# Smaller first transfers in another order, a first weight tile split by chunks, and twelve turns of the identity on TensorE

## The chip, the cores and the metric

The kernel runs on one core of one Trainium2 chip. Its time is the device time of one execution in microseconds (us), and lower is better. The engines of the core are TensorE (PE in the profile), VectorE (DVE), ScalarE (ACT), GpSimd (POOL) and SyncE (SP), which issues most of the transfers. Each runs its own list of instructions in order and waits for the others on semaphores.

## The reference

Two decoder layers over 256 tokens of width 1024, all in float32. Layer 0 mixes tokens by native sparse attention (NSA), layer 1 by multi-head latent attention, and each is followed by a SwiGLU channel mixer. RMS norms stand around every part:

```python
for i in range(DEPTH):                       # DEPTH = 2
    u = rms_norm(h, ln_mix_pre[i])
    m = nsa_mixer(u, ...) if i == 0 else mla_mixer(u, ...)
    h = h + rms_norm(m, ln_mix_post[i])
    u = rms_norm(h, ln_ffn_pre[i])
    h = h + rms_norm(swiglu(u, w_gate, w_up, w_down), ln_ffn_post[i])
```

The NSA mixer begins with `h @ w_in` (keys, values, gates and queries), and turns queries and keys by rotary angles computed from the positions. Only this beginning is touched by the change.

## The kernel before

**Token and weight tiles.** The 256 tokens are two token tiles, t = 0 and 1, with 128 tokens on the partitions. The width is eight chunks of 128. Weights stream through three slots: weight tile n lies in `raw[n % 3]` (128x2048), four chunks of 512 columns for this stage. Tiles 0 and 1 hold the first key/value block (chunks 0 to 3 and 4 to 7), tiles 2 and 3 the second, 4 and 5 the third; then come the gates and the rest.

**Split in two parts.** For float32 accuracy each operand is a rounded high part and a remainder. ScalarE writes `w_hi` (`split_hi`, L229), VectorE writes `w_lo = raw - w_hi` (`split_lo`, L241), and a product is three matmuls (`product`, L256 to L258). `split_hi` counts `hi_ready`, `split_lo` counts `lo_ready`, on which TensorE (`take`) and the load of a slot's next tile wait.

**Activations.** `u = h * gain` is made on VectorE (`pre_norm`, L412), in halves of 512 columns. TensorE turns each half with four transposes (`turn_pe`, L467), ScalarE copies the high part (`turn_act`, L476) and VectorE the low part (`turn_dve`, L482). The norm's root isn't in u: squares and a square root on ScalarE (`pre_root`, L323, L311, L312) and the inverse on VectorE (`pre_invert`, L378 to L384) give a factor that is applied when results leave PSUM (L1166).

**First block on TensorE** (`first_block`): turn both halves of token tile 0; chunks 0 to 7 for token tile 0, with the first half of token tile 1 turned before chunk 6 and the second after chunk 7; chunks 0 to 7 for token tile 1. Then `kv_block(1)` takes tiles 2 and 3 (24 matmuls each), 16 transposes of the keys and values follow (they need the copies at L1166), and `kv_block(2)` takes tiles 4 and 5.

**Order on the other engines.** It is the order in which the code is written. VectorE computes the rotary angles after the inverse roots (L1645 to L1664), ScalarE takes sine and cosine (L1313, L1314), then the high part of tile 3, then the copies at L1166. SP issues x (token tile 0), the gain, tile 0, x (token tile 1), tiles 1 and 2; the load of tile 3 waits for w_lo of tile 0. GpSimd makes the identity for the transposes (L644, L646) after two small transfers.

Of the kernel before, what the change touches and what calls it, by code (L numbers as in the profile page):

```python
# [25 lines left out]
P = 128  # L26
# [80 lines left out]
def trunk(nc, x, positions, inv_freq, gains, lat_gain, nsa_w_in, pe_k, pe_v, w1_k, w1_v, w2_k, w2_v, nsa_w_out,  # L107
          mla_w_in, w_q_up, w_kv_up, mla_w_out, w_gate_up, w_down, out):
    with ExitStack() as ctx:
# [165 lines left out]
        def project_wide(pe, n, stat_hi, stat_lo, first, start, stop, last_of=None):  # L275

            s = n % 3
            for t in range(T):
# [6 lines left out]
                if last_of is not None and t == 0:  # L285
                    last.then_inc(sem(f"acc_done{last_of}"), 1)
# [21 lines left out]
        def root(tally, s, t, k, name):  # L308
# [4 lines left out]
                           bias=stat(s, t, k + 2)).then_inc(sem(f"{name}{s}"), 1)  # L313

        def pre_root(tally, s, t):

            act = tally.eng
            for half in range(2):
                if s == 0:
                    act.wait_ge(sem(f"x_loaded{t}"), 16)  # L320
# [6 lines left out]
        def post_root(tally, s, t, n):  # L327

            act = tally.eng
            if t == 0:  # L330
                act.wait_ge(sem(f"acc_done{s}"), 1)
            else:
                wait_used(act, n)
            for half in range(2):
# [57 lines left out]
        def post_invert(tally, s, t):  # L392
            tally.eng.wait_ge(sem(f"post_root{s}"), t + 1)
# [164 lines left out]
        def _(sp):  # L558
# [80 lines left out]
        def _(pool):  # L639
            pool.memset(eps[:], EPS).then_inc(sem("eps"), 1)  # L640
            pool.dma_start(pos_i[:], positions).then_inc(sem("pos_loaded"), 16)
            pool.dma_start(invf[:], inv_freq.to_broadcast([P, 16])).then_inc(sem("pos_loaded"), 16)

# [3 lines left out]
                               pattern=[[-1, P]], channel_multiplier=1).then_inc(sem("ident"), 1)  # L647

# [66 lines left out]
        def _(pe):  # L715
# [43 lines left out]
            def first_block(s, n):  # L759
# [7 lines left out]
                for t in range(T):  # L767
                    for k in range(KC):
                        if k % 4 == 0:
                            pe.wait_ge(sem(f"u{s}_lo"), 2 * t + k // 4 + 1)  # L770
                            if t == 0:
                                take(pe, n + k // 4)
                        if t == 0 and k == 6:
# [7 lines left out]
                    if t == 0:  # L781
                        last.then_inc(sem(f"first_block{s}"), 1)
# [1092 lines left out]
```

## Time and profile before

| | |
|---|---|
| median of 3 runs | 796.91 us (796.35 to 799.35) |
| profiled execution | span 796.9 us from the first to the last instruction; nothing further is recorded around it |
| TensorE busy | 715.8 us (90%) |
| VectorE busy | 438.9 us (55%) |
| ScalarE busy | 369.6 us (46%) |
| mean granted TensorE clock | 0.951 of full speed |
| chain that ended last | PE 73%, DVE 14%, ACT 6%, issue 5%, DMA 1% |
| moved from memory | 109.54 MB, mean 139 GB/s |

A matmul is pipelined with the next one, so its duration is longer than the distance between two starts: 0.39 us against 0.23 for 512 columns at the full clock. Where two matmuls are compared, the distance of their starts counts. The rows name a line of the kernel; `x4` at the end of a row merges four like instructions. The idle time in brackets is that engine's, ahead of the row, with what ended it.

### The profile page before, as it was taken

To read this page: it belongs to the slowest core of one execution; us is meant where nothing else is said; L and a number is where in the kernel's file an instruction comes from. 1 tells how busy PE (TensorE), PEld (TensorE's weight loads), DVE (VectorE), ACT (ScalarE), POOL (GpSimd) and SP (SyncE) were. 2 spreads that over 40 slices of the span, in tenths; PEclk is the share of its full clock that TensorE was granted. 3 is DMA by queue.
4 is the path that set the end of the run, shared out by engine and by line. 5 is a ranking of instruction groups with operands and counts; after the bars stand their busy time and mean duration, and the time that the engine had idled before them with its cause. 6 is when DMAs were issued, how large, how long until landed. Compare 5 with 4: busy or idle time off the path is not lost.

```text
span 796.9 us, 10320 instructions
## 1 busy us (share of the span) xinstructions
PE 715.8 (90%) x3601; PEld 599.7 (75%) x3601; DVE 438.9 (55%) x898; ACT 369.6 (46%) x678; POOL 75.5 (9%) x63
## 2 busy tenths in 40 slices
PE   3999899938969999999997997887969999999994
PEld 2899787827857888888886787876757888888883
DVE  4666566495386555444556554555285455444553
ACT  6564554505355444334445445445355444334432
POOL 6000011080020000000002001112420000000000
PEclk9999899969989999999999979999999999999998
DMA  9563110431045546554453322242333545654421
GB/s 319 202 210 103 56 40 13 159 109 50 1 152 173 177 163 217 208 201 158 158 190 133 113 87 86 87 134 78 106 127 111 185 161 213 209 206 158 158 106 53
DMA packets 55918, 110.95 MB, mean 139 GB/s; under 512 B 4225, under 2 KB 15537, under 8 KB 55889
## 3 DMA queue, kind: packets, MB, share of 16 engines
q1 hardware_dynamic: 54544, 106.24, 39.5%
q0 software_dynamic: 1344, 4.35, 1.6%
q8 instruction: 15, 0.25, 0.1%
q14 instruction: 15, 0.11, 0.0%
HBM read 109.54 MB, written 1.05 MB: 139 GB/s over the span
## 4 chain that ended last, share of the span: by engine, by line
PE 73%; DVE 14%; ACT 6%; issue 5%; DMA 1%; DVEq 0%; SPq 0%; ACTq 0%
PE bank L256 22%; PE bank L257 21%; PE bank L258 21%; DVE w_lo L241 2%; PE bank L804 2%; PE bank L827 1%; DVE u L412 1%; ACT w_hi L229 1%; PE bank L740 1%; DMA raw<-in_nsa_w_in 1%; PE bank L810 1%; DVE lat_g L1569 1%; DVE nmax L1521 1%; DVE s_sb L1516 1%; DVE h L402 1%
## 5 line engine op out<-in xcount | busy, mean ns | idle before, releaser
L241 DVE TENSOR_TENSOR w_lo<-raw,w_hi 128x2048 fp32r<-128x2048 f32 (+5 forms) x105 | 205.9, 1981 | 65.5 <-ACT w_hi L229 65.4
L256 PE MATMUL bank<-w_hi,act_lo 128*128 128x512 f32 (+3 forms) x592 | 230.7, 390 | 10.9 <-DVE w_lo L241 9.8
L258 PE MATMUL bank<-w_hi,act_hi 128*128 128x512 f32 (+3 forms) x592 | 225.0, 380 | 0.0
L257 PE MATMUL bank<-w_lo,act_hi 128*128 128x512 f32 (+3 forms) x592 | 224.6, 379 | 0.0
L229 ACT ACTIVATE w_hi<-raw 128x2048 fp32r<-128x2048 f32 (+5 forms) x98 | 170.3, 1763 | 20.4 <-PE bank L258 18.6
L256 PEld LDWEIGHTS bank<-w_hi,act_lo 128*128 128x128 f32 x592 | 115.4, 195 | 33.3 <-issue 6.1
L258 PEld LDWEIGHTS bank<-w_hi,act_hi 128*128 128x128 f32 x592 | 115.3, 195 | 20.9
L257 PEld LDWEIGHTS bank<-w_lo,act_hi 128*128 128x128 f32 x592 | 115.5, 195 | 18.7
L1163 ACT ACTIVATE hidT_hi<-bank 128x512 fp32r<-128x512 f32 x22 | 13.1, 597 | 176.3 <-PE bank L740 176.3
L1490 DVE TENSOR_TENSOR hidT_lo<-bank,hidT_hi 128x512 fp32r<-128x512 f32 x22 | 15.2, 692 | 139.9 <-ACT hidT_hi L1163 139.9
L256 PE MATMUL bank<-w_hi,hidT_lo 128*128 128x512 f32 x176 | 69.2, 393 | 3.0 <-DVE hidT_lo L1490 3.0
L257 PE MATMUL bank<-w_lo,hidT_hi 128*128 128x512 f32 x176 | 69.3, 394 | 0.0
L258 PE MATMUL bank<-w_hi,hidT_hi 128*128 128x512 f32 x176 | 68.4, 389 | 0.0
L241 POOL TENSOR_TENSOR w_lo<-raw,w_hi 128x2048 fp32r<-128x2048 f32 x9 | 41.2, 4579 | 270.7 <-ACT w_hi L229 269.7
L1220 ACT ACTIVATE s_sb<-s_sb,nmax 128x128 f32<-128x128 f32 (+1 forms) x72 | 32.4, 451 | 43.4 <-DVE nmax L1521 43.0
L804 PE MATMUL bank<-big,qT 96*128 96x256 f32 (+4 forms) x128 | 46.9, 454 | 5.5 <-DVE big L1613 3.0
L827 PE MATMUL bank<-big,pT 128*128 (+1 forms) x288 | 42.4, 277 | 7.6 <-DVE qs L541 5.0
L827 PEld LDWEIGHTS bank<-big,pT 128*128 128x128 f32 x288 | 40.0, 203 | 10.5 <-DVE qs L541 5.4
L1163 ACT ACTIVATE pT<-bank 128x256 f32<-128x256 f32 (+2 forms) x64 | 25.9, 405 | 37.0 <-PE bank L810 36.8
L256 PEld LDWEIGHTS bank<-w_hi,hidT_lo 128*128 128x128 f32 x176 | 33.0, 188 | 10.9 <-issue 3.4
L1516 DVE CUSTOM_DVE_ANT_0 s_sb<-bank,mask 128x128 f32<-128x128 f32 (+1 forms) x72 | 23.6, 353 | 30.5 <-issue 30.5
L236 POOL CAST w_hi<-raw 128x768 fp32r<-128x768 f32 (+4 forms) x16 | 18.8, 1189 | 226.9 <-PE bank L258 226.9
(184 smaller groups left out, 823.2 us busy)
## 6 DMA issues: line engine op xcount, KB each, us to landing
raw<-in_w_gate_up SPq DMA_DIRECT2D x44, 1024.0 KB, 5.3
raw<-in_w_down SPq DMA_DIRECT2D x22, 1024.0 KB, 5.0
raw<-in_nsa_w_in SPq DMA_DIRECT2D x6, 1024.0 KB, 9.7
raw<-in_w_q_up SPq DMA_DIRECT2D x8, 576.0 KB, 4.3
raw<-in_nsa_w_out SPq DMA_DIRECT2D x4, 1024.0 KB, 6.0
raw<-in_mla_w_in SPq DMA_DIRECT2D x4, 1024.0 KB, 5.1
raw<-in_mla_w_out SPq DMA_DIRECT2D x4, 1024.0 KB, 5.2
gain<-in_gains POOLq DMA_DIRECT2D x7, 512.0 KB, 5.9
```

Of the source, the lines that this page charges most:

```text
L229: act.activation(w_hi[s][:, 0:width], raw[s][:, 0:width], ACT.Copy).then_inc(hi_ready, 1)
L236: pool.tensor_copy(w_hi[s][:, 0:width], raw[s][:, 0:width]).then_inc(hi_ready, 1)
L241: dve.tensor_tensor(w_lo[s][:, 0:width], raw[s][:, 0:width], w_hi[s][:, 0:width].bitcast(F32), ALU.subtract).then_inc(lo_ready, 1)
L256: pe.matmul(dst, a_lo, b_hi, start=start, stop=False)
L257: pe.matmul(dst, a_hi, b_lo, start=False, stop=False)
L258: return pe.matmul(dst, a_hi, b_hi, start=False, stop=stop)
L804: pe.matmul(dst, q, k, start=True, stop=True).then_inc(sem(f"{m}_scores"), 1)
L827: last = pe.matmul(bank[4 if t == 0 else 7][:, b * KVW + i * HD:b * KVW + (i + 1) * HD], p, v, start=kt == 0, stop=kt == t)
L1163: return act.activation(dst, src, ACT.Copy)
L1220: ins = act.activation(v, v, ACT.Exp, bias=nmax[:, n % 3, b:b + 1], scale=scale, accum_out=rsum[:, t, i, b + 1:b + 2])
L1490: dve.tensor_tensor(hidT_lo[:].rearrange("p c s -> p (c s)"), bank[2][:], hidT_hi[:].rearrange("p c s -> p (c s)").bitcast(F32), ALU.subtr ...
L1516: ins = dve.tensor_tensor_reduce(places[m][n % 3][:, b * keys:(b + 1) * keys], bank[n % 2][:, b * keys:(b + 1) * keys], mask[:, SEQ - keys ...
```

## The change

Transfers: x of token tile 0 and the gain come in two halves of 512 columns each, and weight tile 0 in its four chunks. SP's order is x half 0, gain half 0, chunk 0, x half 1, gain half 1, chunks 1, 2, 3, tile 1, x of token tile 1, tile 2. ScalarE and VectorE split tile 0 chunk by chunk (`first_hi`, `first_lo`), and TensorE waits for each chunk alone. The identity is made before GpSimd's first two transfers, and TensorE turns it twelve times into bank 7, where nobody reads it. Several semaphores that were one for each sub-layer become one with a running count (`acc_done`, `half_squared`, `first_block`, `pre_root`, `post_root`). ScalarE and VectorE do the start in another order.

```diff
+        def first_hi(act, c):
+            act.wait_ge(loaded[0] if c == 3 else sem(f"first{c}_loaded"), 16)
+            act.activation(w_hi[0][:, c * 512:(c + 1) * 512], raw[0][:, c * 512:(c + 1) * 512], ACT.Copy) \
+                .then_inc(hi_ready if c == 3 else sem("first_hi"), 1)
+
+        def first_lo(dve, c):
+            if c == 3:
+                dve.wait_ge(hi_ready, 1)
+            else:
+                dve.wait_ge(sem("first_hi"), c + 1)
+            cols = slice(c * 512, (c + 1) * 512)
+            dve.tensor_tensor(w_lo[0][:, cols], raw[0][:, cols], w_hi[0][:, cols].bitcast(F32), ALU.subtract) \
+                .then_inc(lo_ready if c == 3 else sem("first_lo"), 1)
...
-            sp.dma_start(h[:, 0, :], x[0:P, :]).then_inc(sem("x_loaded0"), 16)
-            sp.dma_start(gain[:, 0, :], gains[0:1, :].to_broadcast([P, D])).then_inc(sem("first_gain_loaded"), 16)
+            for half in range(2):
+                cols = block_cols(512 * half, 512)
+                sp.dma_start(h[:, 0, cols], x[0:P, cols]).then_inc(sem(f"x_half{half}_loaded"), 16)
+                sp.dma_start(gain[:, 0, cols], gains[0:1, cols].to_broadcast([P, 512])) \
+                    .then_inc(sem(f"gain_half{half}_loaded"), 16)
+                for c in ((0,), (1, 2, 3))[half]:
+                    sp.dma_start(raw[0][:, c * 512:(c + 1) * 512], nsa_w_in[c * P:(c + 1) * P, D:D + 512]) \
+                        .then_inc(loaded[0] if c == 3 else sem(f"first{c}_loaded"), 16)
...
-            pool.dma_start(pos_i[:], positions).then_inc(sem("pos_loaded"), 16)
-            pool.dma_start(invf[:], inv_freq.to_broadcast([P, 16])).then_inc(sem("pos_loaded"), 16)
-
             pool.memset(ident[:], 0.0).then_inc(sem("ident0"), 1)
             pool.wait_ge(sem("ident0"), 1)
             pool.affine_select(out=ident[:], in_=ident[:], compare_op=ALU.not_equal, fill=1.0, base=0,
                                pattern=[[-1, P]], channel_multiplier=1).then_inc(sem("ident"), 1)
+            pool.dma_start(pos_i[:], positions).then_inc(sem("pos_loaded"), 16)
+            pool.dma_start(invf[:], inv_freq.to_broadcast([P, 16])).then_inc(sem("pos_loaded"), 16)
...
-                            if t == 0:
+                            if t == 0 and (s > 0 or k > 0):
                                 take(pe, n + k // 4)
+                        if s == 0 and t == 0 and k < 3:
+                            pe.wait_ge(sem("first_lo"), k + 1)
+                        elif s == 0 and t == 0 and k == 3:
+                            take(pe, n)
...
+            for _ in range(12):
+                pe.transpose(bank[7][:, 0:P], ident[:], ident[:])
...
+            first_hi(act, 0)
+            turn_act(act, "u0", 0, [0])
+            first_hi(act, 1)
+            turn_act(act, "u0", 0, [1])
+            first_hi(act, 2)
+            first_hi(act, 3)
+            split_hi(act, 1, SLOT)
+            turn_act(act, "u0", 1, [0])
             pre_root(chain, 0, 0)
-            turn_act(act, "u0", 0)
-            split_hi(act, 0, SLOT)
+            turn_act(act, "u0", 1, [1])
+            split_hi(act, 2, SLOT)
             pre_root(chain, 0, 1)
-            split_hi(act, 1, SLOT)
-            split_hi(act, 2, SLOT)
-            turn_act(act, "u0", 1)
...
-            turn_dve(dve, "u0", 0)
-            split_lo(dve, 0, SLOT)
+                first_lo(dve, half)
+                turn_dve(dve, "u0", 0, [half])
+            first_lo(dve, 2)
+            first_lo(dve, 3)
+            split_lo(dve, 1, SLOT)
             dve.wait_ge(sem("x_loaded1"), 16)
             for half in range(2):
                 pre_norm(dve, 0, 1, half)
-            split_lo(dve, 1, SLOT)
+            turn_dve(dve, "u0", 1)
             split_lo(dve, 2, SLOT)
-            turn_dve(dve, "u0", 1)
             pre_invert(chain, 0)
```

ScalarE before, from the squares of token tile 1 on (L323 squares, L311 and L312 the root, L229 the high part of a weight tile, L476 a turn's high part). The first L229 row is tile 1, the next tile 2, the last tile 3:

```order
L323 ACTIVATE s_sb,stats<-h 128x512 [waits x_loaded1]
L323 ACTIVATE s_sb,stats<-h 128x512 [waits x_loaded1,act_chain]
L311 ACTIVATE stats<-stats 128x1 [waits act_chain]
L312 ACTIVATE stats<-stats 128x1 [waits act_chain]
L229 ACTIVATE w_hi<-raw 128x2048 [waits slot1_loaded]
L229 ACTIVATE w_hi<-raw 128x2048 [waits slot2_loaded]
L476 ACTIVATE act_hi<-bank 128x4x128 [waits u0_turned] x2
L1313 ACT_TABLE_LOAD
L1313 ACTIVATE sin<-ang 128x48 [waits angles]
L1314 ACTIVATE cos<-ang 128x48
L229 ACTIVATE w_hi<-raw 128x2048 [waits weights_used,slot0_loaded]
```

ScalarE now, after the high part of tile 1 (L488 is the turn's high part, L337 the squares, L325 and L326 the root; the L229 row is tile 2):

```order
L488 ACTIVATE act_hi<-bank 128x4x128 [waits u0_turned]
L337 ACTIVATE s_sb,stats<-h 128x512 [waits x_half0_loaded]
L337 ACTIVATE s_sb,stats<-h 128x512 [waits x_half1_loaded,act_chain]
L325 ACTIVATE stats<-stats 128x1 [waits act_chain]
L326 ACTIVATE stats<-stats 128x1 [waits act_chain]
L488 ACTIVATE act_hi<-bank 128x4x128 [waits u0_turned]
L229 ACTIVATE w_hi<-raw 128x2048 [waits slot2_loaded]
L337 ACTIVATE s_sb,stats<-h 128x512 [waits x_loaded1]
L337 ACTIVATE s_sb,stats<-h 128x512 [waits x_loaded1,act_chain]
L325 ACTIVATE stats<-stats 128x1 [waits act_chain]
L326 ACTIVATE stats<-stats 128x1 [waits act_chain]
L1346 ACT_TABLE_LOAD
```

Both turns of token tile 1 and token tile 0's squares and root moved ahead of tile 2, and token tile 1's squares and root moved behind it. The sine, the cosine and tile 3 follow the last row as before.

VectorE before, from the turns of token tile 0 on (L412 is u, L241 w_lo, L482 a turn's low part, L378 the first reciprocal of the inverse roots):

```order
L482 TENSOR_TENSOR act_lo<-bank,act_hi 128x4x128 [waits u0_hi] x2
L241 TENSOR_TENSOR w_lo<-raw,w_hi 128x2048 [waits hi_ready]
L412 TENSOR_TENSOR u<-h,gain 128x512 [waits first_gain_loaded,x_loaded1]
L412 TENSOR_TENSOR u<-h,gain 128x512 [waits first_gain_loaded]
L241 TENSOR_TENSOR w_lo<-raw,w_hi 128x2048 [waits hi_ready] x2
L482 TENSOR_TENSOR act_lo<-bank,act_hi 128x4x128 [waits u0_hi] x2
L378 RECIPROCAL stats<-stats 128x1 [waits pre_root0]
```

VectorE now, after chunks 0 and 1 (L263 is w_lo of chunks 2 and 3, L424 u, L494 a turn's low part, L390 the first reciprocal):

```order
L494 TENSOR_TENSOR act_lo<-bank,act_hi 128x4x128 [waits u0_hi]
L263 TENSOR_TENSOR w_lo<-raw,w_hi 128x512 [waits first_hi]
L263 TENSOR_TENSOR w_lo<-raw,w_hi 128x512 [waits hi_ready]
L241 TENSOR_TENSOR w_lo<-raw,w_hi 128x2048 [waits hi_ready]
L424 TENSOR_TENSOR u<-h,gain 128x512 [waits x_loaded1]
L424 TENSOR_TENSOR u<-h,gain 128x512
L494 TENSOR_TENSOR act_lo<-bank,act_hi 128x4x128 [waits u0_hi] x2
L241 TENSOR_TENSOR w_lo<-raw,w_hi 128x2048 [waits hi_ready]
L390 RECIPROCAL stats<-stats 128x1 [waits pre_root]
```

W_lo of tile 2 moved from before the two turns of token tile 1 to behind them, directly ahead of the inverse roots and the angles.

## Rows read from the trace of the kernel before

**Rows 1.** The page: TensorE's busy time (part 1) and its busy tenths (part 2).

```profile
PE 715.8 (90%) x3601; PEld 599.7 (75%) x3601; DVE 438.9 (55%) x898; ACT 369.6 (46%) x678; POOL 75.5 (9%) x63
...
PE   3999899938969999999997997887969999999994
```

**Rows 2.** Chain of waits, first 45 us: start us, us, what.

```profile
1.73 9.09 DMA raw<-in_nsa_w_in
...
10.84 1.92 ACT w_hi L229
...
12.78 2.30 DVE w_lo L241
...
15.22 0.77 PE bank L256
```

**Rows 3.** Timeline of PE: start us, us, engine, line, op, tiles, [idle before <-releaser].

```profile
7.58 1.94 PE L467 MATMUL bank<-ident,u 128*128 128x128 f32 x8 [7.58 <-DVE u L412]
...
17.92 0.63 PE L256 MATMUL bank<-w_hi,act_lo 128*128 128x512 f32 x1
...
18.35 0.63 PE L257 MATMUL bank<-w_lo,act_hi 128*128 128x512 f32 x1
...
19.97 0.40 PE L256 MATMUL bank<-w_hi,act_lo 128*128 128x512 f32 x1
...
21.36 0.60 PE L467 MATMUL bank<-ident,u 128*128 128x128 f32 x4
...
34.54 0.39 PE L256 MATMUL bank<-w_hi,act_lo 128*128 128x512 f32 x1
```

**Rows 4.** Timeline of ACT, first 31 us.

```profile
12.66 0.61 ACT L323 ACTIVATE s_sb<-h 128x512 f32<-128x512 f32 x1
...
14.83 1.91 ACT L229 ACTIVATE w_hi<-raw 128x2048 fp32r<-128x2048 f32 x1 [0.15 <-DMA raw<-in_nsa_w_in]
...
21.99 0.60 ACT L476 ACTIVATE act_hi<-bank 128x512 fp32r<-128x512 f32 x1 [2.38 <-PE bank L467]
...
29.84 0.24 ACT L1313 ACTIVATE sin<-ang 128x48 f32<-128x48 f32 x1 [4.13 <-DVE ang L1664]
...
30.12 1.90 ACT L229 ACTIVATE w_hi<-raw 128x2048 fp32r<-128x2048 f32 x1
```

**Rows 5.** Timeline of DVE, first 33 us.

```profile
6.64 1.40 DVE L412 TENSOR_TENSOR u<-h,gain 128x512 f32<-128x512 f32 x2 [6.64 <-DMA gain<-in_gains]
...
24.45 0.69 DVE L482 TENSOR_TENSOR act_lo<-bank,act_hi 128x512 fp32r<-128x512 f32 x1 [1.13 <-ACT act_hi L476]
...
25.06 0.15 DVE L378 RECIPROCAL stats<-stats 128x1 f32<-128x1 f32 x1
...
32.06 2.29 DVE L241 TENSOR_TENSOR w_lo<-raw,w_hi 128x2048 fp32r<-128x2048 f32 x1 [2.25 <-ACT w_hi L229]
```

**Rows 6.** Windows: stretch, length, busy by engine, PEclk, DMA share, GB/s.

```profile
0.00:7.00 7.00, 0.00 (x0) 0.00 (x0) 0.36 (x1) 3.43 (x8) 5.41 (x19) 1.00 0.67 193
...
7.00:15.00 8.00, 1.94 (x8) 1.57 (x8) 4.64 (x6) 5.10 (x10) 7.49 (x15) 1.00 1.05 379
...
4.00:6.00 2.00, 0.00 (x0) 0.00 (x0) 0.00 (x0) 1.76 (x6) 2.00 (x5) 1.00 0.84 187
```

**Rows 7.** Timeline of PE after two later waits.

```profile
222.34 0.50 PE L256 MATMUL bank<-w_hi,act_lo 128*128 128x512 f32 x1 [1.77 <-DVE w_lo L241]
...
222.68 0.39 PE L257 MATMUL bank<-w_lo,act_hi 128*128 128x512 f32 x1
...
595.27 0.66 PE L467 MATMUL bank<-ident,u 128*128 128x128 f32 x4 [4.28 <-DVE u L412]
...
596.63 0.63 PE L258 MATMUL bank<-w_hi,act_hi 128*128 128x512 f32 x1
...
599.61 0.39 PE L256 MATMUL bank<-w_hi,act_lo 128*128 128x512 f32 x1
```

**Rows 8.** Timeline of POOL, the identity.

```profile
3.04 0.29 POOL L646 TENSOR_SCALAR_AFFINE_SELECT ident<-ident 128x128 f32<-128x128 f32 x1 [0.24 <-POOL ident L644]
```

More of the change, by code:

```diff
@@ L285, in project_wide @@
                 if last_of is not None and t == 0:
-                    last.then_inc(sem(f"acc_done{last_of}"), 1)
+                    last.then_inc(sem("acc_done"), 1)
             last.then_inc(weights_used, 1)
@@ L319, in pre_root @@
                 if s == 0:
-                    act.wait_ge(sem(f"x_loaded{t}"), 16)
+                    act.wait_ge(sem("x_loaded1") if t else sem(f"x_half{half}_loaded"), 16)
                 else:
@@ L330, in post_root @@
             if t == 0:
-                act.wait_ge(sem(f"acc_done{s}"), 1)
+                act.wait_ge(sem("acc_done"), s + 1)
             else:
@@ L342, in post_root @@
                 if t == 0 and half == 0:
-                    ins.then_inc(sem(f"half_squared{s}"), 1)
-                    act.wait_ge(sem(f"half_squared{s}"), 1)
+                    ins.then_inc(sem("half_squared"), 1)
+                    act.wait_ge(sem("half_squared"), s + 1)
                 else:
@@ L349, in wait_gain @@
         def wait_gain(dve, k):
-            if k == 0:
-                dve.wait_ge(sem("first_gain_loaded"), 16)
-            else:
+            if k > 0:
                 dve.wait_ge(sem(f"gain{k % 4}_loaded"), 16 * (k // 4 + (k % 4 != 0)))
@@ L358, in gained @@
             if t == 0:
-                dve.wait_ge(sem(f"acc_done{s}"), 1)
+                dve.wait_ge(sem("acc_done"), s + 1)
             else:
@@ L365, in gained @@
                 if t == 0 and half == 0:
-                    dve.wait_ge(sem(f"half_squared{s}"), 1)
+                    dve.wait_ge(sem("half_squared"), s + 1)
                 cols = slice(half * 512, (half + 1) * 512)
@@ L583, in block_cols @@
                 return slice(lo, lo + n)
-            sp.dma_start(h[:, 0, :], x[0:P, :]).then_inc(sem("x_loaded0"), 16)
-            sp.dma_start(gain[:, 0, :], gains[0:1, :].to_broadcast([P, D])).then_inc(sem("first_gain_loaded"), 16)
+            for half in range(2):
[6 more added lines that the diff above has]
+                        .then_inc(loaded[0] if c == 3 else sem(f"first{c}_loaded"), 16)
             for b in range(3):
                 for half in range(2):
+                    if b == 0 and half == 0:
+                        continue
                     load(NSA_KV + 2 * b + half, rows(nsa_w_in, 4 * half, 4, block_cols(D + 512 * b, 512)))
-                    if b == 0 and half == 0:
+                    if b == 0 and half == 1:
                         sp.dma_start(h[:, 1, :], x[P:2 * P, :]).then_inc(sem("x_loaded1"), 16)
@@ L781, in first_block @@
                     if t == 0:
-                        last.then_inc(sem(f"first_block{s}"), 1)
+                        last.then_inc(sem("first_block"), 1)
                         turn_half(1, 1)
@@ L1069, in output @@
                         if half == 1 and t == 0:
-                            last.then_inc(sem(f"acc_done{s}"), 1)
+                            last.then_inc(sem("acc_done"), 1)
             attend("nsa", 0, None, opening=True)
@@ L1186, in gated @@
                             if t == 0:
-                                act.wait_ge(sem(f"first_block{s}"), 1)
+                                act.wait_ge(sem("first_block"), s + 1)
                             else:
@@ L1628, in rotate @@
                          sem("mla_roped"))
-            dve.wait_ge(sem("x_loaded0"), 16)
             for half in range(2):
+                dve.wait_ge(sem(f"x_half{half}_loaded"), 16)
+                dve.wait_ge(sem(f"gain_half{half}_loaded"), 16)
                 pre_norm(dve, 0, 0, half)
-            turn_dve(dve, "u0", 0)
-            split_lo(dve, 0, SLOT)
+                first_lo(dve, half)
[3 more added lines that the diff above has]
+            split_lo(dve, 1, SLOT)
             dve.wait_ge(sem("x_loaded1"), 16)
```

6 lines of the change are left out of this document (3 added, 3 removed).

## The prediction

> **What bounds the kernel now.** I read the page first, then the chain of waits over the start, then the timelines of TensorE, ScalarE and VectorE there, then windows for the DMA rate. The page has TensorE busy for 715.8 of 796.9 us, and after its second slice it is nearly full [rows 1]. So a change that touches only the start can win at most what TensorE waits there, and keeps it only if everything that feeds TensorE moves forward with it.
>
> The chain of waits shows the start: tile 0 of the weights lands at 10.82, ScalarE rounds it (1.92), VectorE subtracts (2.30), and TensorE's first product starts at 15.22 [rows 2]. From there it is continuous: tile 1's first product (token tile 0, chunk 4) is at 19.97, and the fourth weight tile (tile 3) begins at 34.54 [rows 3]. The first products are 0.43 us apart (512 columns at 1.2 GHz) and last 0.63, the later ones last 0.39 and are 0.23 apart (the 2.4 GHz level; 24 of tile 2 and 24 of token tile 1 take 5.5 each): 9.5 of the first 12 pay 0.2 us more, about 2 us.
>
> The second thing to see is how late w_lo of tile 3 is. VectorE starts it at 32.06 and takes 2.29, so it is ready at 34.35, and TensorE asks for it at 34.5 [rows 3, 5]. There is no slack. What it hangs on is a chain with little to do with weights: VectorE begins the inverse roots at 25.06, after the activations of token tile 1, goes on to the rotary angles, ScalarE takes sine and cosine at 29.84, only then rounds tile 3 (30.12), and VectorE subtracts [rows 4, 5]. From the first reciprocal to w_lo of tile 3 it is 34.35 - 25.06 = 9.29 us.
>
> **The change part by part.**
>
> *Transfers.* Half of x, half of the gain and one chunk come first. Before, VectorE waited for both whole transfers until 6.64, TensorE turned u from 7.58 [rows 3, 5]. Halved, I take u's first half at about 5 and the second, which needs the second gain half, at about 8; chunks 0 to 3 land up to 10.8, where tile 0 landed as a whole, since the bytes ahead of its end are the same. TensorE can then do chunks 0 to 3 of token tile 0 from about 9.5 on, each as its 512 columns are split (ScalarE about 0.6, VectorE about 0.7, as for the same width in rows 4 and 5). The last is ready near 12.3. So these 12 products, 4.75 us before (15.22 to 19.97), vanish behind transfers. Of the 4.75 at most what tile 1 allows becomes visible.
>
> *Tile 1 is the new first bound.* It now goes ahead of x's second half (0.52 MB), not behind it. The moved bytes ahead of its end are 3.15 MB. Windows give 1.35 MB in the first 7 us, then 379 GB/s [rows 6]: 3.15 MB at 7 + 1.80/0.379 = 11.75. Tile 0's 2.10 MB are reached by the same count at 8.97, and it landed at 10.82, 1.85 later, since later transfers were moving already. With that lag, 13.6. The low end comes from before: ScalarE took tile 1 at 14.83 after an idle 0.15 [rows 4], so it had landed at 14.2 to 14.8; less 0.52/0.379 = 1.4 for x, 12.8. I take 13.2. Then 1.94 + 2.29 + 0.15, as in rows 2, put its first product, which I call K, at 13.2 + 4.4 = 17.6 (17.2 to 18.0), against 19.97. That is the gain, 2.4 us, if nothing else gave way.
>
> *ScalarE's and VectorE's new order takes it back.* ScalarE now has, after tile 1: turn of token tile 1 (half 0), squares and root of token tile 0, turn (half 1), tile 2, squares and root of token tile 1, sine. Before, the squares and tile 2 lay in ScalarE's idle time ahead of the turns at 21.99 (its 2.38 of idle is in the row) [rows 4]; now they stand behind the first turn. Call B the moment ScalarE starts that turn. Then:
> - turn 0.52 (start to next start), squares and root 14.83 - 0.15 - 12.66 = 2.02, turn 0.52: tile 2 starts at B + 3.1, ends B + 5.0
> - VectorE's w_lo of tile 2, now ahead of the inverse roots: 0.05 + 2.29, to B + 7.3
> - root of token tile 1 on ScalarE by B + 7.0: hidden behind it. The load of the sine's table is behind that and hidden by the angles
> - reciprocal at B + 7.3, and the chain of 9.29: w_lo of tile 3 at B + 16.6, product at B + 16.7.
>
> B: in the trace the turn starts 21.99 - 19.97 = 2.02 after K's product at the high clock (six products and four transposes lie between). So tile 3 starts at 17.6 + 2.0 + 16.7 = 36.3, against 34.54: **1.8 later**. TensorE itself would be there at K + 34.54 - 19.97 = 32.2, so it now idles some 4 us. What follows (tiles 3, 4, 5, the copies of the keys and their loads, all behind tile 3 on ScalarE and VectorE) shifts alike: tile 4 and 5 were ready early only because they followed tile 3 directly, and still do. I found no later wait with slack that could absorb it, as TensorE is the bound [rows 1].
>
> *Clock.* Two idle stretches are new: about 3 us ahead of K (chunk 3 done near 13.6 to 14.5, K at 17.6) and 4 us ahead of tile 3. In the trace a wait of 4.28 us ends with products of 0.63 us, the low level's, and the first of 0.39, the high level's, comes 4.3 us later; after a wait of 1.77 they are of 0.39 at once [rows 7]. So the second stretch costs about half of 4.3, 2.1 us (0 to 2.7). The first, if the clock is down at K, makes six products cost 6 x 0.2 and four transposes 0.24 each, not 0.11 (1.94 for 8 against 0.60 for 4 less overlap [rows 3]), and delays the second turn a little: 1.2 + 0.4 + 0.4 = 2.0 on the chain. It can stay up, since 12 products at the low rate now fill most of 9.5 to 14. The Trainium skill, in "TensorE: Matmul & The Clock Gate", Part 1, has it that the throttled level is the default and activity lifts it; by that, both new pauses are an expense that the change's twelve turns of the identity cannot pay for, as they end long before. The 4.28 us row agrees; no row shows a pause of 3 us.
>
> *Twelve turns.* TensorE waits for ident, which POOL finished at 3.3 [rows 8] behind two DMA issues that now come after it, so I put it near 2.0. At 0.24 each they end near 5, before u. They cost nothing (at most 0.3 if u's first half is there at 4.6), and also gain nothing, as the products they precede are hidden. The merged semaphores change no order: nothing. The extra SP issues (five more at 0.42, so tile 2 is issued near 5.3) are ahead of the data: nothing. POOL's DMAs for positions are used at 27: nothing.
>
> **Sum.** +1.8 with no loss of clock; +3.8 or +3.9 with one of the two; +5.9 with both. The profiled span is 796.9 and the median of the runs 796.91, so they are one base. One loss is likeliest: 800.8. As both losses are likelier than none, I write **801.0**.
>
> **Rivals.**
> - *Both clock losses*: 802.8. For it: 3 us of idle may be enough, and two pauses come within 20 us. Against: the short pause of rows 7.
> - *None*: 798.7. For it: the level could be up until a little into each pause. Against: the 4.28 us row.
> - *Faster*: tile 1's lead survives, because the angles chain is shorter than I add, or tile 3 is ready by 32.2. Then 19.97 - 17.6 = 2.4 less: 794.5. It decides at w_lo of tile 3 before 34.35, so B at 17.7 or earlier, which needs tile 1 landed at 11.3; the bytes of rows 6 do not allow it.
> - *Pieces are slow*: while the gain came in, windows show 187 GB/s [rows 6]: a broadcast row read by all partitions. If halves cost what the whole did, tile 1 lands 2.5 later: 803.5. The Trainium skill, in "DMA: Bandwidth & Descriptors", Bandwidth, advises 1 MiB transfers, since each has some 2 us of fixed cost; taken one after the other, the pieces would come out far later still. The trace speaks against it: SP's transfers of before overlap fully from 7 us on.
> - *The change does nothing visible* (796.9): if two errors of mine meet; part of "same".
>
> **How the numbers follow.** One loss 0.42, both 0.30, none 0.14, slow pieces 0.06, faster 0.05, nothing 0.03. 0.5% of 796.9 is 4.0 us, about what a measurement here tells from no change; a time over 800.9 is slower. One loss lies on the line: half of it each way, 0.21. Slower 0.21 + 0.30 + 0.06 = 0.57, same 0.21 + 0.14 + 0.03 + 0.02 = 0.40, the 0.02 being the part of "faster" that stays within 4 us; 0.03 is left beyond. Range 798.0 to 803.6: none to both, and 0.7 to 0.8 on each side for K (0.4) and for what a clock loss costs. That leaves out about 0.15.
>
> **What would show it.** Twelve transposes ending by 5; chunk 0's first product at 9 to 10; tile 1's at 17.2 to 18.0; ScalarE's tile 2 after the second turn, near 22.7 to 25; reciprocal near 27 to 29; TensorE idle 3.5 to 4.5 ahead of tile 3, whose first product is at 36 to 38.5, and products 0.43 apart behind it. From there on an even shift to the end. I am wrong if tile 3's product starts at or before 34.5, or if a later wait swallows the shift.

## The result and the profile after

| | before | changed |
|---|---|---|
| median of 10 runs each, same chip | 797.91 us (791.90 to 800.14) | 801.71 us (799.38 to 808.76) |
| ratio of the times | | 1.0074, 95% interval 1.0046 to 1.0101 |
| profiled execution, span | 796.9 us | 806.1 us |
| mean granted TensorE clock | 0.951 | 0.941 |

The changed kernel is slower by 0.74%, 5.9 us on the 796.91 of the prediction (3.7 to 8.0 by the interval); the two medians are 3.8 us apart, at the low end of it. The times of single runs lie 1.7 to 2.7 us over their spans. The profiled run of the changed kernel took 808.76, 7 over its median, so its span says too much of the change; its start can be read to a tenth of a us.

TensorE's busy time of the page after (to [rows 1]):

```profile
PE 725.3 (90%) x3613; PEld 606.4 (75%) x3613; DVE 438.7 (54%) x901; ACT 370.2 (46%) x681; POOL 74.9 (9%) x63
...
PE   5899899948969999999997997887979999999994
```

TensorE's timeline after, with the columns of [rows 3], which it answers. L940 are the twelve turns of the identity, L479 the turns of u, L270 to L272 the three matmuls of a product:

```profile
1.63 2.82 PE L940 MATMUL bank<-ident 128*128 128x128 f32 x12 [1.63 <-POOL ident L665]
6.67 1.12 PE L479 MATMUL bank<-ident,u 128*128 128x128 f32 x4 [2.21 <-DVE u L424]
...
10.62 0.78 PE L270 MATMUL bank<-w_hi,act_lo 128*128 128x512 f32 x1
...
14.89 0.39 PE L272 MATMUL bank<-w_hi,act_hi 128*128 128x512 f32 x1
...
18.37 0.77 PE L270 MATMUL bank<-w_hi,act_lo 128*128 128x512 f32 x1 [3.09 <-DVE w_lo L241]
18.93 0.63 PE L271 MATMUL bank<-w_lo,act_hi 128*128 128x512 f32 x1
...
35.62 0.39 PE L272 MATMUL bank<-w_hi,act_hi 128*128 128x512 f32 x1
...
39.11 0.80 PE L270 MATMUL bank<-w_hi,act_lo 128*128 128x512 f32 x1 [3.10 <-DVE w_lo L241]
39.70 0.63 PE L271 MATMUL bank<-w_lo,act_hi 128*128 128x512 f32 x1
...
45.10 0.40 PE L272 MATMUL bank<-w_hi,act_hi 128*128 128x512 f32 x1
```

To be seen: the twelve turns are over at 4.5. Tile 0's products run from 10.6 to 15.2 while tile 1 is loaded and split, so they are hidden. Tile 1 begins at 18.37, 1.6 earlier than the 19.97 of before, but at the low clock (0.63 us a matmul). Tile 3 begins at 39.11, 4.6 later than 34.54, after a new wait of 3.10 us for VectorE's w_lo, and again at the low clock until 45.

ScalarE's timeline after (to [rows 4]). L229 at 13.99 is tile 1, L488 the turns of token tile 1, L229 at 25.61 tile 2, L1346 the sine, L229 at 34.83 tile 3:

```profile
13.99 1.91 ACT L229 ACTIVATE w_hi<-raw 128x2048 fp32r<-128x2048 f32 x1 [1.35 <-DMA raw<-in_nsa_w_in]
22.16 0.60 ACT L488 ACTIVATE act_hi<-bank 128x512 fp32r<-128x512 f32 x1 [6.26 <-PE bank L479]
...
25.11 0.60 ACT L488 ACTIVATE act_hi<-bank 128x512 fp32r<-128x512 f32 x1 [0.42 <-PE bank L479]
25.61 1.91 ACT L229 ACTIVATE w_hi<-raw 128x2048 fp32r<-128x2048 f32 x1
...
34.55 0.24 ACT L1346 ACTIVATE sin<-ang 128x48 f32<-128x48 f32 x1 [3.81 <-DVE ang L1700]
...
34.83 1.90 ACT L229 ACTIVATE w_hi<-raw 128x2048 fp32r<-128x2048 f32 x1
```

VectorE's (to [rows 5]): the first reciprocal behind w_lo of tile 2, and w_lo of tile 3.

```profile
27.55 2.29 DVE L241 TENSOR_TENSOR w_lo<-raw,w_hi 128x2048 fp32r<-128x2048 f32 x1 [1.11 <-ACT w_hi L229]
29.75 0.16 DVE L390 RECIPROCAL stats<-stats 128x1 f32<-128x1 f32 x1
...
36.76 2.29 DVE L241 TENSOR_TENSOR w_lo<-raw,w_hi 128x2048 fp32r<-128x2048 f32 x1 [2.25 <-ACT w_hi L229]
```

ScalarE now idles 6.26 us ahead of the first turn, and all that stood in its idle time before is queued behind it. That is the whole mechanism: tile 2, both roots, the inverse roots, the angles and the sine come one after the other, and tile 3 is behind them.

### The profile page after: what moved, and what is told of

The parts are those of the page before. It is cut to its first block, busy times and chain, and to the rows that moved or that the text cites. A ratio compares the mean times of both kernels' runs of the same rounds, so it can differ in the third digit from the quotient of the medians.

```text
span 806.1 us, 10354 instructions
## 1 busy us (share of the span) xinstructions
PE 725.3 (90%) x3613; PEld 606.4 (75%) x3613; DVE 438.7 (54%) x901; ACT 370.2 (46%) x681; POOL 74.9 (9%) x63
## 4 chain that ended last, share of the span: by engine, by line
PE 71%; DVE 15%; ACT 6%; issue 5%; DMA 1%; SPq 0%; DVEq 0%; ACTq 0%
PE bank L270 22%; PE bank L271 21%; PE bank L272 21%; DVE w_lo L241 3%; PE bank L829 2%; ACT w_hi L229 2%; PE bank L852 1%; DVE u L424 1%; PE bank L761 1%; DMA raw<-in_nsa_w_in 1%; PE bank L835 1%; DVE lat_g L1602 1%; DVE nmax L1554 1%; PE bank L479 1%; DVE h L414 1%
## 5 line engine op out<-in xcount | busy, mean ns | idle before, releaser
L270 PE MATMUL bank<-w_hi,act_lo 128*128 128x512 f32 (+3 forms) x592 | 234.4, 396 | 11.4 <-DVE w_lo L241 10.3
L241 DVE TENSOR_TENSOR w_lo<-raw,w_hi 128x2048 fp32r<-128x2048 f32 (+5 forms) x104 | 203.6, 1978 | 67.6 <-ACT w_hi L229 67.5
L271 PE MATMUL bank<-w_lo,act_hi 128*128 128x512 f32 (+3 forms) x592 | 227.3, 384 | 0.0
L272 PE MATMUL bank<-w_hi,act_hi 128*128 128x512 f32 (+3 forms) x592 | 227.2, 384 | 0.0
L229 ACT ACTIVATE w_hi<-raw 128x2048 fp32r<-128x2048 f32 (+5 forms) x97 | 168.4, 1761 | 19.6 <-PE bank L272 18.1
L270 PEld LDWEIGHTS bank<-w_hi,act_lo 128*128 128x128 f32 x592 | 117.2, 198 | 34.6 <-DVE w_lo L241 8.9
L272 PEld LDWEIGHTS bank<-w_hi,act_hi 128*128 128x128 f32 x592 | 116.7, 197 | 21.5
L271 PEld LDWEIGHTS bank<-w_lo,act_hi 128*128 128x128 f32 x592 | 117.3, 198 | 19.0
L1191 ACT ACTIVATE hidT_hi<-bank 128x512 fp32r<-128x512 f32 x22 | 13.2, 598 | 176.2 <-PE bank L761 176.2
L1523 DVE TENSOR_TENSOR hidT_lo<-bank,hidT_hi 128x512 fp32r<-128x512 f32 x22 | 15.2, 692 | 139.9 <-ACT hidT_hi L1191 139.9
L270 PE MATMUL bank<-w_hi,hidT_lo 128*128 128x512 f32 x176 | 69.2, 393 | 3.0 <-DVE hidT_lo L1523 3.0
L272 PE MATMUL bank<-w_hi,hidT_hi 128*128 128x512 f32 x176 | 68.4, 389 | 0.0
L241 POOL TENSOR_TENSOR w_lo<-raw,w_hi 128x2048 fp32r<-128x2048 f32 x9 | 41.1, 4570 | 275.0 <-ACT w_hi L229 274.1
L270 PEld LDWEIGHTS bank<-w_hi,hidT_lo 128*128 128x128 f32 x176 | 33.0, 188 | 10.9 <-issue 3.4
```

The costliest lines, as they stand in the source:

```text
L229: act.activation(w_hi[s][:, 0:width], raw[s][:, 0:width], ACT.Copy).then_inc(hi_ready, 1)
L241: dve.tensor_tensor(w_lo[s][:, 0:width], raw[s][:, 0:width], w_hi[s][:, 0:width].bitcast(F32), ALU.subtract).then_inc(lo_ready, 1)
L270: pe.matmul(dst, a_lo, b_hi, start=start, stop=False)
L271: pe.matmul(dst, a_hi, b_lo, start=False, stop=False)
L272: return pe.matmul(dst, a_hi, b_hi, start=False, stop=stop)
L1191: return act.activation(dst, src, ACT.Copy)
```

## The experiments

Ten kernels ran, each against the kernel before on the same chip. Since single runs of one kernel scatter by 1 to 1.5%, the first thing read in each is the start in its trace. This table gathers it; the rows behind it follow one by one. Times in us from the start of the span; "turn" is ScalarE's first turn of token tile 1, "w_lo 3" the start of VectorE's part of tile 3, "wait" what stands ahead of tile 3's first product.

| kernel | tile 1 | turn | w_lo 3 | tile 3 | wait | ratio to before (95%) |
|---|---|---|---|---|---|---|
| before | 19.97 | 21.99 | 32.06 | 34.54 | none | |
| changed | 18.37 | 22.16 | 36.76 | 39.11 | 3.10 | 1.0074 (1.0046 to 1.0101) |
| e1_old_order | 18.54 | 23.50 | 34.02 | 37.60 | none | 1.0028 (0.9993 to 1.0064) |
| e2_only_order | 20.58 | 22.72 | 36.76 | 39.10 | 3.42 | 1.0058 (1.0025 to 1.0092) |
| e3_no_turns | 18.57 | 22.36 | 36.73 | 39.07 | 3.10 | 1.0067 (1.0032 to 1.0103) |
| e4_early_angles | 18.66 | 22.45 | 33.02 | 35.90 | none | 1.0021 (0.9988 to 1.0053) |
| e5_filled_wait | 18.75 | 20.84 | 34.89 | 37.24 | 3.42 | 1.0072 (1.0043 to 1.0100) |
| e6_all | 18.47 | 20.57 | 29.06 | 33.12 | none | 1.0004 (0.9979 to 1.0029) |
| e7_whole_gain | 18.79 | 22.44 | 36.49 | 38.84 | 3.47 | 1.0060 (1.0039 to 1.0082) |
| e8_orders_only | 18.29 | 21.35 | 30.47 | 34.52 | none | 1.0009 (0.9983 to 1.0034) |
| e9_before_angles | 19.57 | 21.58 | 29.62 | 34.12 | none | 1.0012 (0.9977 to 1.0046) |
| e10_before_filled | 19.11 | 21.21 | 29.26 | 33.76 | none | 0.9969 (0.9939 to 0.9998) |

### e1: the changed kernel with the old order

```diff
 split_hi(act, 1, SLOT)
-turn_act(act, "u0", 1, [0])
 pre_root(chain, 0, 0)
-turn_act(act, "u0", 1, [1])
-split_hi(act, 2, SLOT)
 pre_root(chain, 0, 1)
+split_hi(act, 2, SLOT)
+turn_act(act, "u0", 1)
...
-turn_dve(dve, "u0", 1)
 split_lo(dve, 2, SLOT)
+turn_dve(dve, "u0", 1)
```

> The changed kernel with ScalarE and VectorE put back from tile 1 on: after tile 1 ScalarE does both squares and roots, then tile 2, then both turns of token tile 1; VectorE does w_lo of tile 2 ahead of the turns. New transfers, chunks and the twelve turns stay. Theory (the new order puts the inverse roots and the angles behind tile 2): the first product of tile 1 stays at 18.4, the reciprocal moves from 29.8 to about 26.1, w_lo of tile 3 is ready at about 35.4, tile 3's first product at 35.9 instead of 39.1 with no wait ahead of it, and the second stretch at the low clock (38.1 to 44.9) goes with the wait: about 5 us less than the changed kernel's profiled 806.1, in the median 1 to 2 us over the kernel before. Rival (the small transfers are what costs, by the later landing of tile 1): tile 3 at 38 or later and the time stays 4 to 6 us over before.

Half of it came true. The wait ahead of tile 3 is gone, and the ratio falls to 1.0028. Its interval holds no change, but it also overlaps with the changed kernel's, so the times alone don't tell e1 from either. But tile 3 is at 37.60, not 35.9. Tile 2 had not landed: ScalarE waited for it until 21.67, where the kernel before had it at 17.70, and both turns stand behind it. TensorE then waits for token tile 1's low parts. ScalarE's row for tile 2, in the kernel before and in e1, and two of TensorE in e1:

```profile
17.70 1.91 ACT L229 ACTIVATE w_hi<-raw 128x2048 fp32r<-128x2048 f32 x1 [0.96 <-DMA raw<-in_nsa_w_in]
```

```profile
21.67 1.92 ACT L229 ACTIVATE w_hi<-raw 128x2048 fp32r<-128x2048 f32 x1 [1.74 <-DMA raw<-in_nsa_w_in]
```

```profile
26.57 0.49 PE L270 MATMUL bank<-w_hi,act_lo 128*128 128x512 f32 x1 [2.63 <-DVE act_lo L494]
...
37.60 0.39 PE L270 MATMUL bank<-w_hi,act_lo 128*128 128x512 f32 x1
```

So the new transfers have a price of their own that the new order hides: tile 2 comes 4 us later. With the new transfers the old order doesn't fit.

Where the 4 us come from can be read, though it wasn't tried by itself. SP's queue (q1) needs 4.72 MB up to the end of tile 2. By 16 us it had moved 4.60 MB before and 4.31 in e1. Then GpSimd's queue (q0) brings the later gains, issued from 12.94 before and from 11.56 in e1, and takes most of the bandwidth. The two queues from 16 to 20 us (packets, MB, share of the 16 engines), before and then e1:

```profile
q0 software_dynamic: 353, 1.32, 83.1%
q1 hardware_dynamic: 162, 0.30, 20.4%
```

```profile
q0 software_dynamic: 287, 1.04, 66.3%
q1 hardware_dynamic: 288, 0.56, 37.3%
```

Before, 0.12 MB of tile 2 were left for this stretch, in e1 0.41 MB, and SP's queue moved only 0.14 MB a us in it. At that rate 0.41 MB take 3 us. Tile 3's load shares SP's queue with it, released at 13.2 in e1 (15.1 before) by w_lo of tile 0. So a lag of 0.3 MB, 0.8 us at the full rate, became 4 us.

### e2: the kernel before with only the new order

```diff
-pre_root(chain, 0, 0)
 turn_act(act, "u0", 0)
 split_hi(act, 0, SLOT)
-pre_root(chain, 0, 1)
 split_hi(act, 1, SLOT)
-split_hi(act, 2, SLOT)
-turn_act(act, "u0", 1)
+turn_act(act, "u0", 1, [0])
+pre_root(chain, 0, 0)
+turn_act(act, "u0", 1, [1])
+split_hi(act, 2, SLOT)
+pre_root(chain, 0, 1)
```

VectorE's calls are in the changed kernel's order too.

> The kernel before with only the new order on ScalarE and VectorE from tile 0 on; transfers, split of tile 0 and identity as before. Theory: first product of tile 1 stays near 20.0, w_lo of tile 3 comes 16.6 us after the first turn of token tile 1 (22.0), so tile 3's first product is at 38.7 instead of 34.5: 4.2 us slower, and 6 to 7 where the clock falls in the wait of 4 us. Rival (the order alone is harmless and only does damage together with a late tile 1 at the low clock): within 1 us of before.

Tile 3 came at 39.10 (38.7 expected, with tile 1 at 20.0; it was at 20.58), after a wait of 3.42:

```profile
39.10 0.79 PE L256 MATMUL bank<-w_hi,act_lo 128*128 128x512 f32 x1 [3.42 <-DVE w_lo L241]
```

The changed kernel's is 39.11, and the time is slower beyond its interval (1.0058). The order alone is enough for the loss, with no transfer touched. The rival is out. That the two agree to 0.01 us is chance: the first turn is at 22.72 here and at 22.16 there, but there the second turn waited 0.42 us for TensorE, and tile 2 follows at 25.63 and 25.61.

### e3: without the twelve turns

```diff
-for _ in range(12):
-    pe.transpose(bank[7][:, 0:P], ident[:], ident[:])
```

> The changed kernel without the twelve turns of the identity. Theory: they end at 4.5, the first products they might warm run at the low level anyway until 14.2, and these are hidden behind tile 1's landing: tile 1's first product within 0.2 us of 18.4 and the time the same as the changed kernel's (0.5 to 1% over before). Rival (they raise the clock in time for chunks 0 to 3 and their loss is felt): chunk products of the first block end later, beyond 15.3, but tile 1 still at 18.4; or (they cost something) 1 us faster.

Tile 1 at 18.57 and tile 3 at 39.07, as with the turns; the ratio is 1.0067 against 1.0074. They do nothing for the products. In two of the seven traces that have them (e1 and e7) the clock did rise: the first turn of u behind them took 0.66 us for its four matmuls, against 1.12 in the changed kernel and 1.09 here. But in both it had fallen again by 8.5 us, ahead of the products. By the way, after the same wait of 3.10 us the clock was still high in this run:

```profile
39.07 0.50 PE L270 MATMUL bank<-w_hi,act_lo 128*128 128x512 f32 x1 [3.10 <-DVE w_lo L241]
39.41 0.40 PE L271 MATMUL bank<-w_lo,act_hi 128*128 128x512 f32 x1
```

A wait of that length costs the clock in some executions and not in others.

### e4: the changed kernel with the angles earlier

```diff
+<the twelve instructions of the rotary angles>
 turn_dve(dve, "u0", 1)
 split_lo(dve, 2, SLOT)
 pre_invert(chain, 0)
-<the twelve instructions of the rotary angles>
```

> The changed kernel with VectorE's rotary angles moved from behind the inverse roots to ahead of the turns of token tile 1, where VectorE idled 3.36 us. ScalarE's order stays. Theory: ScalarE takes the sine right behind token tile 1's root (29.4) and the table load, at about 30.7 instead of 34.5; w_lo of tile 3 ready at about 35.3, TensorE reaches tile 3 at 35.8 without a wait: about 5 us less than the changed kernel's profiled 806.1, 1 to 2 over before. Rival (tile 3 waits on something else, its transfer or its slot): tile 3 stays at 38 to 39.

Sine at 30.80 (30.7 expected), tile 3 at 35.90 (35.8 expected), without a wait:

```profile
30.80 0.24 ACT L1346 ACTIVATE sin<-ang 128x48 f32<-128x48 f32 x1
```

```profile
35.90 0.39 PE L270 MATMUL bank<-w_hi,act_lo 128*128 128x512 f32 x1
```

The transfer and the slot of tile 3 had been there; the angles were what it waited for. Tile 3 is still 1.4 us later than before, though tile 1 was 1.3 earlier: from tile 1 to tile 3 it took 17.24 us and not 14.57, with no wait between, so the 2.7 us are the low clock behind tile 1. As in e1, the ratio's interval overlaps with the changed kernel's; it is the start that shows the repair.

### e5: TensorE's wait for tile 1 filled

```diff
+if s == 0 and t == 0 and k == 4:
+    for _ in range(24):
+        pe.transpose(bank[7][:, 0:P], ident[:], ident[:])
```

> The changed kernel with 24 more turns of the identity on TensorE between chunk 3 and chunk 4, in its wait for tile 1 (15.1 to 18.4; 24 at 0.11 us are 2.6 at the high clock, 5.6 at the low). Theory (the pause ahead of tile 1 drops the clock, and the low clock moves the first turn of token tile 1 and with it tile 3): tile 1's first product stays at 18.4 to 18.6 but the products behind it are 0.23 apart, the first turn is at 20.6 instead of 22.2, tile 3's first product at 37.3 instead of 39.1, still with a wait of 4 us ahead of it, in which the clock may fall: 1 to 4 us less than the changed kernel. Rival (the clock falls for another reason, as the mix of work, not the pause): products 0.43 apart behind 18.4 and tile 3 at 39.

```profile
15.19 2.78 PE L792 MATMUL bank<-ident 128*128 128x128 f32 x24
18.75 0.47 PE L270 MATMUL bank<-w_hi,act_lo 128*128 128x512 f32 x1 [0.78 <-DVE w_lo L241]
19.06 0.40 PE L271 MATMUL bank<-w_lo,act_hi 128*128 128x512 f32 x1
...
37.24 0.50 PE L270 MATMUL bank<-w_hi,act_lo 128*128 128x512 f32 x1 [3.42 <-DVE w_lo L241]
```

In the trace all came as the theory has it: high clock behind 18.75, turn at 20.84 (20.6), tile 3 at 37.24 (37.3). So the pause had lowered the clock; e6, filled likewise, is high there too, while all six traces with the unfilled pause are low at tile 1 or fall within a us. The time doesn't follow: 1.0072, no better than the changed kernel's. The intervals are 0.3% wide to each side, and 1.9 us are 0.24%; it is inconclusive on the time.

### e7: the gain in one transfer

```diff
-for each half: gain[:, 0, cols] <- gains[0:1, cols]
+once, behind x's first half: gain[:, 0, :] <- gains[0:1, :]
```

> The changed kernel with the gain in one transfer again (behind x's first half), everything else as changed. It tells what halving it costs: tile 1 landed at 13.97 where the same bytes and the old lag gave 13.2 to 13.6. If halves of a broadcast row are slower: tile 1 lands 0.5 earlier, its product at 17.9. If not: still 18.4, and u's first half is 0.7 to 1 later (6.6 to 7.0 instead of 5.9). The time is that of the changed kernel within 1 us either way, since the chain behind tile 1 is the same.

Tile 1 was taken at 14.40 (changed: 13.99), the first half of u started at 6.10 (5.92). Both are no earlier with the whole gain, so nothing shows that halving it costs, and the bound for slow halves falls. Neither came as expected, though: u's first half wasn't 0.7 to 1 later. The seven traces with the halved gain took tile 1 at 13.77 to 14.36. Tile 3 is at 38.84.

The first us differ between the kernels, but they don't explain the landing of tile 1. Windows of 2 to 4 us, before, changed, and e7:

```profile
2.00:4.00 2.00, 0.00 (x0) 0.00 (x0) 0.00 (x0) 0.29 (x2) 1.62 (x5) 1.00 0.98 322
```

```profile
2.00:4.00 2.00, 2.00 (x11) 2.00 (x10) 0.00 (x0) 0.29 (x2) 2.00 (x4) 1.00 0.97 227
```

```profile
2.00:4.00 2.00, 2.00 (x11) 2.00 (x10) 0.00 (x0) 0.29 (x2) 2.00 (x4) 1.00 1.05 304
```

95 GB/s less over 2 us are 0.19 MB, 0.5 us at 379 GB/s. With the gain whole the rate is back at 304 GB/s, and tile 1 still comes no earlier. Why it lands later than the bytes ahead of it say is open. Nor is a broadcast row slow in itself, as [rows 6] might suggest with 187 GB/s: from 16 to 20 us before, GpSimd's queue, with gains of the same kind, moved 1.32 of 1.62 MB, at 406 GB/s in all.

### e8 and e6: both orders mended, without and with the filled wait

```diff
 split_hi(act, 1, SLOT)
-turn_act(act, "u0", 1, [0])
 pre_root(chain, 0, 0)
-turn_act(act, "u0", 1, [1])
-split_hi(act, 2, SLOT)
 pre_root(chain, 0, 1)
+turn_act(act, "u0", 1)
+split_hi(act, 2, SLOT)
...
 first_lo(dve, 3)
+<the twelve instructions of the rotary angles>
 split_lo(dve, 1, SLOT)
```

> e6 without the 24 filling turns: only the two orders are mended. Theory: tile 1's first product at 18.8 at the low clock, tile 3 at 36.0 without a wait ahead of it: 1.5 over before. Against e6 it tells what the clock alone is worth: 2 to 2.6 us at tile 3. Rival (the clock of the start is a matter of chance and the filling does not steer it): e6 and e8 alike.

> The changed kernel with three repairs: the rotary angles ahead of w_lo of tile 1 on VectorE; on ScalarE both squares and roots right behind tile 1, both turns, then tile 2; and the 24 filling turns of e5. Theory: tile 1's first product at 18.8 (the angles cost w_lo of tile 1 up to 0.3), tile 2's w_lo at 27.5 just in time, tile 3 needs nothing late and starts 14.6 after tile 1, at 33.4, 1.1 before the kernel before's 34.5: median 1 us under before, which its scatter may not tell from no change. Rival (a next wait stands right behind): tile 3 at 34.5 or later.

e8 first, then e6, tile 3's first product:

```profile
34.52 0.39 PE L270 MATMUL bank<-w_hi,act_lo 128*128 128x512 f32 x1
```

```profile
33.12 0.39 PE L270 MATMUL bank<-w_hi,act_lo 128*128 128x512 f32 x1
```

e6 is 0.3 ahead of what was expected and 1.4 ahead of before. e8 was expected at 36.0 and came at 34.52: tile 1 itself was 0.5 earlier, and in this execution the clock stayed high until 19.2 and was back at 22.6, so it lost less. From tile 1 to tile 3 it took 16.2 us and e6 14.65, so the clock is worth 1.6 us between the two, not 2 to 2.6. Both are back at the time of before (1.0009 and 1.0004), and their intervals end below that of the changed kernel, so both are faster than it. The gain of 1.4 us of e6 (0.18%) is below what the times resolve.

### e9 and e10: the same two ideas on the kernel before

```diff
 turn_dve(dve, "u0", 1)
+<the twelve instructions of the rotary angles>
 pre_invert(chain, 0)
-<the twelve instructions of the rotary angles>
```

e10 adds 22 turns of the identity into bank 7, ahead of TensorE's first product.

> The kernel before with only the rotary angles ahead of the inverse roots on VectorE (2.75 us of work changes places with 1.9). It asks whether the angles bound anything before the change. Theory (TensorE and w_lo of tile 3 arrived together at 34.5, so an earlier w_lo wins nothing): w_lo of tile 3 ready at 32.4 to 32.6 instead of 34.35, tile 3's first product still 14.6 after tile 1's (34.5), time the same. Rival (the chain was binding already): tile 3 earlier, 1 to 2 us faster.

> e9 with 22 turns of the identity on TensorE ahead of its first product, in the wait for tile 0 (9.5 to 15.2; 22 at 0.24 us are 5.3). Theory: the clock is high at 15.2, the 12 products of tile 0 take 2.7 instead of 4.75 us, then tile 1 (w_lo ready at 19.1) is waited for: its first product at 19.2 instead of 20.0, tile 3's at 33.8, 0.8 under before: not to be told from no change in the medians. Rival (turns of 128 columns do not lift the clock): products 0.43 apart from 15.2 on and no gain.

In e9 w_lo of tile 3 started at 29.62, and tile 3's product was at 34.12, 14.55 after tile 1's: the same distance as before (34.54 - 19.97 = 14.57). The angles bound nothing before the change. One of its twelve runs took 1412.9 us and is left out of the ratio; why isn't known. e10:

```profile
9.10 4.30 PE L769 MATMUL bank<-ident 128*128 128x128 f32 x22
15.13 0.47 PE L256 MATMUL bank<-w_hi,act_lo 128*128 128x512 f32 x1 [1.73 <-DVE w_lo L241]
15.44 0.39 PE L257 MATMUL bank<-w_lo,act_hi 128*128 128x512 f32 x1
...
19.11 0.47 PE L256 MATMUL bank<-w_hi,act_lo 128*128 128x512 f32 x1 [0.98 <-DVE w_lo L241]
...
33.76 0.39 PE L256 MATMUL bank<-w_hi,act_lo 128*128 128x512 f32 x1
```

The turns lift the clock, tile 1 is at 19.11 (19.2 expected) and tile 3 at 33.76 (33.8). Its median is 795.41 against 797.91, ratio 0.9969, the lowest of all. Its interval ends at 0.9998, one of eleven such intervals, so that it beats the kernel before isn't safe. The start shows 0.8 us (0.10%); that the rest is real isn't shown.

## Why the prediction was right or wrong

**The sign and the chain were right.** Slower was the likeliest, and the median 801.71 is inside the range. What was written of the chain held to tenths: from the turn to w_lo of tile 3 it was 36.76 - 22.16 = 14.6 (14.3 forecast: 16.6 less the 2.29 of w_lo itself). e2 shows that the order alone does it, e4 that the angles are the link.

That the median is only 0.7 from the forecast of 801.0 is luck in part. The forecast was 4.1 over a base of three runs; the base of ten runs was 1.0 higher, and the ratio says 5.9. Of the marks set ahead, the twelve turns over by 5 and the low clock behind tile 3 were met. The times were missed to the late side: first product of tile 0 at 10.62 (9 to 10), tile 1 at 18.37 (17.2 to 18.0), ScalarE's tile 2 at 25.61 (22.7 to 25), reciprocal at 29.75 (27 to 29), tile 3 at 39.11 (36 to 38.5). TensorE idled 3.10 ahead of it (3.5 to 4.5), since the low clock had made TensorE itself late.

**The step that failed: when ScalarE starts the turn (B).** Against the base of 796.9 I had 0.51%, and 0.74% was measured. Tile 3 was forecast at 36.3 and came 2.8 later: 0.8 by K, 1.8 by the low clock between K and B, 0.2 by the chain behind B. The two terms of the sum that were short:
- *K, the landing of tile 1.* I took 13.2 and the first product at 17.6, at most 18.0. It was 13.99 and 18.37. The count of bytes with the lag of 1.85 gave 13.6, and I went below it, towards a bound from a wait of 0.15 us. The rest, up to 0.8 us, is open (e7). The term "2.4 us earlier" measured 1.6.
- *The clock.* I made one loss the likeliest (0.42) and both 0.30. The profiled execution has both: low from 18.37 on, with the turn 3.79 after tile 1's product and not 2.02, and again behind 39.11. Of the five further kernels with the unfilled pause, four (e1, e3, e4, e7) started tile 1 at the low level and the fifth (e8) fell to it a us later, so I should have put that loss at nearly 1. The second is open each time: low at once in the changed kernel and in e2, still high in e3, and it fell 0.4 us later in e7 and 1.2 later in e5. From tile 3 to 49 us the distance to the trace of before grew by 2.7 us in the changed kernel (2.1 in the sum), by 1.6 in e5 and e7, and not at all in e3.

With K as measured and the low clock ahead of the turn, the sum is 18.37 + 3.79 + 16.7 = 38.9, 4.3 over 34.54, and 2 more where the clock falls behind it: 6.3. That is inside the measured 3.7 to 8.0, which doesn't tell 4.3 from 6.3; and as the next paragraphs show, the shift of the start isn't carried to the end unaltered.

**The profiled execution isn't the median.** The forecast set its sum on 796.9, the median then and the span of the profiled run. As single times lie 1.7 to 2.7 over the span, that execution probably took 799.35, the first of the three times. The reason given for the base (the span is the time) was wrong; the base itself was the median of three runs, 1.0 under that of the ten.

**Not foreseen: the shift isn't even.** "From there on an even shift to the end" failed. Traces of before and after are 4.7 us apart at w_lo of tile 3, 7.4 at 49 us, 5.0 to 5.4 from 96 to 510, 3.5 at 534, and 9.2 at the end. No later wait swallowed the 2 us between 49 and 96; the mean granted clock there was lower before (0.85) than in the same part of the changed kernel (0.93):

```profile
49.00:96.00 47.00, 42.47 (x293) 39.20 (x291) 30.96 (x69) 25.98 (x49) 0.00 (x0) 0.85 0.32 92
```

```profile
56.00:102.00 46.00, 40.61 (x299) 37.63 (x298) 30.95 (x70) 27.03 (x52) 0.00 (x0) 0.93 0.32 93
```

So when the low stretches fall depends on more than the start: at 220 us the changed kernel is 5.2 behind before and e2 5.0, but e3, with the same start to 0.04 us, 2.1. The last step is in 560 to 605, where the mean granted clock was 0.94 before and 0.85 after. Windows, before and then changed:

```profile
560.00:605.00 45.00, 38.55 (x180) 30.86 (x179) 24.12 (x41) 22.61 (x47) 11.35 (x3) 0.94 0.35 117
```

```profile
560.00:605.00 45.00, 36.42 (x153) 28.86 (x152) 20.00 (x40) 20.01 (x38) 13.72 (x3) 0.85 0.28 94
```

The instructions there are the same in both kernels. From 534 us to the end the distance to the trace of before grows by 5.7 us in the changed kernel, by 5.0 in e6, 4.9 in e1, 2.8 in e7 and e3, and not at all in e2 and e5, though e2 has tile 3 where the changed kernel has it. So it doesn't come from the start; I take it for scatter of the clock there, without a test of its own. It is why a profiled span can't be compared to better than some 5 us here.

**The rest.** The twelve turns did nothing for the time, as forecast (e3). Slow pieces: halving the gain shows no cost (e7), and on GpSimd's queue broadcast rows moved faster than 187 GB/s. "Faster" failed at the point named for it: tile 1 would have had to land at 11.3. What I did not see is that tile 2 lands 4 us later with the new transfers, as GpSimd's gains are on their way by then (e1); it is hidden only because the new order asks for it late.

## What to carry to other kernels

Before work is put behind a wait in an engine's list, look at what hangs on the work that stands after it: here a weight tile, two roots and a table of angles one after the other made a chain of 16.7 us that the next weights had to pass. A start that gets earlier only on one operand of the bound engine turns its gain into a pause: in all six traces with an unfilled pause ahead of tile 1 TensorE's clock was low behind it, at once or within a us; idle turns helped right ahead of the products that wait (e5, e6, e10), not when they end 6 us before (e3). A transfer that slips a little can slip a lot, if it slips into what another queue moves (e1). When single runs scatter by more than the effect, compare the start of a named instruction over several traces, and take the ratio of many runs for the rest.

## What the runs showed of the hardware

- After a wait of 3.10 us TensorE's products were at the low level in the changed kernel (0.63 us each) and at the high one in e3 (0.40). After 2.62 us they were low in e7 (tile 1), after 2.63 high in e1 (at 26.57). The level isn't a function of the wait alone.
- 22 transposes of 128 columns (4.3 us) right behind the eight of u lifted the clock from the low level: the products behind them take 0.39 us each in e10, 0.63 in e9 without them. 24 such transposes in 2.8 us held it over the pause ahead of tile 1 (e5, e6).
- The same 3.15 MB landed later than by the rate of before (13.2 to 13.6) when they came in smaller pieces: tile 1 was taken at 13.77 to 14.36 in seven traces with the gain in halves and at 14.40 with it whole.
- Two DMA queues share the engines: while GpSimd's moved 1.32 MB from 16 to 20 us, SP's moved 0.30, though it had work; from 12 to 16 us, nearly alone, it had moved 1.54 (before).
